# A hybrid DeltaNet/Conformer layer: scan output copied out of PSUM before its norm, and one short convolution for all sample rows

## What is computed

```
proj = rmsnorm(x, g_mix) @ w_in                       # q|k|v, z, b, a, GLU input
qkv  = silu(causal_depthwise_conv([history, q|k|v], w_short))   # width 4, 1536 channels
o, s = gated_delta_rule(l2norm(q), l2norm(k), v, g, beta, s0)   # chunked scan, 8 heads x 64
o    = rmsnorm(o, g_o) * silu(z)                      # norm per head of 64
cv   = silu(group_layernorm(causal_depthwise_conv([history, glu], w_dw)))  # width 31
x    = x + concat([o, cv]) @ w_out                    # then an MLP of width 4096 and a gate
```

## Time and profile before

| | |
|---|---|
| median of 3 runs | 1814.85 us (1811.62 to 1817.52) |
| profiled execution, own time | 1815.31 us |
| its span | 1813.5 us |
| TensorE busy | 1619.3 us, 89% |
| VectorE busy | 1042.2 us, 57% |
| ScalarE busy | 749.3 us, 41% |
| chain that ended last, TensorE's share | 68% |
| mean granted TensorE clock | 0.951 |

### The profile page before, as it was taken

The page is one execution under the profiler, slowest core; times in us unless marked ns, Lnnn a source line. Parts: engine busy times, 40 slices in busy tenths (PEclk is TensorE's granted clock), DMA queues, the critical chain, the costliest instruction groups (busy, mean ns, idle before and its releaser), DMA issues.

```text
span 1813.5 us, 27026 instructions
## 1 busy us (share of the span) xinstructions
PE 1619.3 (89%) x11162; PEld 1405.8 (78%) x11162; DVE 1042.2 (57%) x1707; ACT 749.3 (41%) x1192; POOL 65.6 (4%) x68
## 2 busy tenths in 40 slices
PE   4998866899989997877899999987999999999987
PEld 2786656888978775654677777766989999999987
DVE  3755699678763665779655554455334343434543
ACT  5556523344355424532224243354543242414454
POOL 0000000000000040000000000000000000000000
PEclk9999897899999989888899999999999999999999
DMA  6353222322233332312221213323323333233322
GB/s 181 87 146 102 66 79 65 84 81 77 65 104 82 78 87 68 90 47 64 59 68 45 65 52 91 98 83 117 101 83 93 88 88 94 82 94 87 92 70 82
DMA packets 281023, 153.33 MB, mean 85 GB/s; under 512 B 36996, under 2 KB 272636, under 8 KB 280893
## 3 DMA queue, kind: packets, MB, share of 16 engines
q1 hardware_dynamic: 279879, 150.32, 29.3%
q10 hardware_dynamic: 1022, 1.28, 0.3%
HBM read 135.03 MB, written 16.97 MB: 84 GB/s over the span
## 4 chain that ended last, share of the span: by engine, by line
PE 68%; DVE 16%; ACT 8%; issue 4%; DMA 3%; ACTq 0%; SPq 0%; POOL 0%; DVEq 0%; POOLq 0%
PE ps L1299 55%; DVE of L1964 3%; DVE prod L1883 3%; PE ps L1435 2%; DVE Xp L1884 2%; DVE w_lo L1634 2%; PE ps L1464 2%; PE ps L1458 1%; PE ps L1413 1%; DVE tk L1856 1%; ACT L919 1%; DMA w_raw<-in_w_up 1%; PE ps L1282 1%; PE ps L1425 1%; ACT w_hi L915 1%
## 5 line engine op out<-in xcount | busy, mean ns | idle before, releaser
L915 ACT ACTIVATE w_hi<-w_raw 128x1024 fp32r<-128x1024 f32 (+3 forms) x258 | 232.6, 902 | 320.1 <-DMA w_raw<-in_w_down 175.8
L1299 PE MATMUL ps<-hh_hi,w_hi 128*128 128x256 f32 (+1 forms) x960 | 322.4, 336 | 29.0 <-DVE w_lo L1634 23.2
L1299 PE MATMUL ps<-hh_lo,w_hi 128*128 128x256 f32 (+1 forms) x960 | 314.9, 328 | 0.0
L1299 PE MATMUL ps<-hh_hi,w_lo 128*128 128x256 f32 (+1 forms) x960 | 314.3, 327 | 0.0
L1634 DVE TENSOR_TENSOR w_lo<-w_raw,w_hi 128x1024 fp32r<-128x1024 f32 (+3 forms) x258 | 266.7, 1034 | 55.1 <-ACT w_hi L915 54.3
L1299 PE MATMUL ps<-u_hi,w_hi 128*128 128x512 f32 (+2 forms) x768 | 260.3, 339 | 28.6 <-DVE w_lo L1634 14.2
L1299 PE MATMUL ps<-u_lo,w_hi 128*128 128x512 f32 (+2 forms) x768 | 252.7, 329 | 0.0
L1299 PE MATMUL ps<-u_hi,w_lo 128*128 128x512 f32 (+2 forms) x768 | 252.2, 328 | 0.0
L1299 PE MATMUL ps<-hm_hi,w_hi 128*128 128x512 f32 (+5 forms) x600 | 211.1, 352 | 27.2 <-ACT yb L961 9.8
L1299 PEld LDWEIGHTS ps<-hh_hi,w_hi 128*128 128x128 f32 x960 | 184.8, 193 | 52.9 <-DVE w_lo L1634 34.1
L1299 PE MATMUL ps<-hm_lo,w_hi 128*128 128x512 f32 (+5 forms) x600 | 201.1, 335 | 0.0
(11 more groups left out here) (274 smaller groups left out, 2254.1 us busy)
## 6 DMA issues: line engine op xcount, KB each, us to landing
w_raw<-in_w_up SPq DMA_DIRECT2D x64, 512.0 KB, 4.0
w_raw<-in_w_in SPq DMA_DIRECT2D x48, 512.0 KB, 4.2
w_raw<-in_w_down SPq DMA_DIRECT2D x64, 256.0 KB, 2.7
w_raw<-in_w_down SPq DMA_DIRECT2D x32, 512.0 KB, 4.0
w_raw<-in_w_out SPq DMA_DIRECT2D x16, 512.0 KB, 4.0
w_raw<-in_w_ple_gate SPq DMA_DIRECT2D x16, 512.0 KB, 4.1
qt<-qkv_dram SPq DMA_DIRECT2D x8, 768.0 KB, 5.2
xin<-in_x_prompt SPq DMA_DIRECT2D x8, 512.0 KB, 6.3
```

What stands on the lines that cost most here:

```text
L915: nc.scalar.activation(w_hi[job.slot][:, 0:job.kts, 0:job.m], w_raw[job.slot][:, 0:job.kts, 0:job.m], ACT.Copy).then_inc(w_hid, 1)
L1299: last = nc.tensor.matmul(dst, wt[job.slot][:, k, 0:m], x[:, k, lo:hi], start=(i == 0 and n == 0), stop=(end and n == 2), skip_group_check ...
```

## The change

**The norm.** In `gsq` ACT now copies the tile's output from PSUM to `onr` in head order, waits for that copy (`o_copied`), and squares `onr` from SBUF. In `gno` DVE multiplies `onr` in place. TensorE's first state-times-Q product of the next tile, which overwrites the output's banks, waits for the copy and no longer for the norm.

**The samples' short convolution.** ACT copies the 32 sample columns of a q|k|v block straight to `raws` (history and new rows of all 12 blocks), and no longer to `raw` and `yb`. DVE's per-block short convolution covers only the 512 prompt tokens. A new stage `sv` does all 12 blocks at once: four products and three sums over 128 x 384 (`sy`, `spr`), one copy of the new history, a Silu on ACT, and one DMA of 12 x 32 columns. It stands where `dc` of block 0 stood; that one moves to the slot of block 1's. `dc` now waits for the DMA of `sy`.

```diff
+    put(half("qkv", 1, QT - 1) + 7, "sv")
     for p in range(CT):
-        put(half("ga", 1, p) + 3, "dc", p)
+        put(half("ga", 1, max(p, 1)) + 3, "dc", p)
...
+            def spill_samples():
+                sp.wait_ge(s_silu, 1)
+                sp.dma_start(qkv_dram.rearrange("(k p) t -> p k t", p=P)[:, :, SEQ:TOK],
+                             sy[:, :, :, :].rearrange("p k b t -> p k (b t)")).then_inc(s_st, 16)
...
-                nc.scalar.activation(raw[j % 2][:, QH + lo:QH + hi], src, ACT.Copy)
-                nc.scalar.activation(yb[n][:, lo:hi], src, ACT.Copy, scale=wsh[:, SC - 1, j:j + 1]).then_inc(freed(job, c), 1)
+                end = min(hi, HALF)
+                nc.scalar.activation(raw[j % 2][:, QH + lo:QH + end], src[:, 0:end - lo], ACT.Copy)
+                if hi > HALF:
+                    nc.scalar.activation(raws[:, j, :, QH:], src[:, HALF - lo:].rearrange("p (b t) -> p b t", b=DB), ACT.Copy).then_inc(s_in, 1)
+                nc.scalar.activation(yb[n][:, lo:end], src[:, 0:end - lo], ACT.Copy, scale=wsh[:, SC - 1, j:j + 1]).then_inc(freed(job, c), 1)
...
+            def sample_silu():
+                act.wait_ge(s_conv, 1)
+                nc.scalar.activation(sy[:, :, :, :], sy[:, :, :, :], ACT.Silu).then_inc(s_silu, 1)
...
                 act.wait_ge(o_mm, GATE[t] + 1)
-                src = ps[:, 4:6, 0:PR * HD] if t < NT else ps[0:NS, 4:5, 0:2 * PR * HD]
-                nc.scalar.activation(sqt[0:n, 0:DW].rearrange("p (a b) -> p a b", a=1 if t == NT else 2), src, ACT.Square).then_inc(o_sq, 1)
+                wait(act, o_tr, GATE[t])
...
+                nc.scalar.activation(dst, src, ACT.Copy).then_inc(o_cp, 1)
+                act.wait_ge(o_cp, GATE[t] + 1)
+                nc.scalar.activation(sqt[0:n, 0:DW], onr[0:n, :], ACT.Square).then_inc(o_sq, 1)
...
                 if b == 0:
-                    wait(pe, o_n, GATE[t])
+                    wait(pe, o_cp, GATE[t])
...
                 for k in range(QH):
-                    if s and k == 0:
-                        step(nc.vector.tensor_copy(raws[:, j, :, QH:QH + DS], x[:, QH + HALF:].rearrange("p (b t) -> p b t", b=DB)))
-                        nc.vector.tensor_copy(tail[:, j, 0:QH], x[:, HALF:HALF + QH])
-                        nc.vector.tensor_copy(tail[:, j, QH:].rearrange("p (b r) -> p b r", b=DB), raws[:, j, :, DS:DS + QH])
-                    elif k == 0:
-                        nc.vector.tensor_copy(qh[:, j, :], x[:, HALF:HALF + QH])
-                    if s:
-                        nc.vector.scalar_tensor_tensor(out=ys, in0=raws[:, j, :, k:k + DS], scalar=w(k), in1=ys, op0=ALU.mult, op1=ALU.add)
+                    if k == 0:
+                        nc.vector.tensor_copy(tail[:, j, 0:QH] if s else qh[:, j, :], x[:, HALF:HALF + QH])
...
+            def sample_conv():
+
+                dve.wait_ge(s_in, QT)
+                for n in range(2):
+                    dve.wait_ge(st_yb[n], 16 * spills(1, "qkv")[n])
+                ys, pr = sy[:, :, :, :], spr[:, :, :, :]
+                for k in range(SC):
+                    w = bc(bc(wsh[:, k, :], 2, DB), 3, DS)
+                    step(nc.vector.tensor_tensor(pr if k else ys, raws[:, :, :, k:k + DS], w, ALU.mult))
+                    if k and k < SC - 1:
+                        step(nc.vector.tensor_tensor(ys, ys, pr, ALU.add))
+                nc.vector.tensor_tensor(ys, ys, pr, ALU.add).then_inc(s_conv, 1)
+                nc.vector.tensor_copy(tail[:, :, QH:].rearrange("p j (b r) -> p j b r", b=DB), raws[:, :, :, DS:DS + QH]).then_inc(s_conv, 1)
...
                 dve.wait_ge(o_r, g + 1)
-                wait(dve, o_tr, g)
...
+                nc.vector.tensor_tensor(heads(onr[0:n, :]), heads(onr[0:n, :]), bc(ss[0:n, 0:H], 2, HD), ALU.mult).then_inc(o_n, 1)
...
             def sample_taps(p):
-                for n in range(2):
-                    dve.wait_ge(st_yb[n], 16 * spills(1, "qkv")[n])
+                dve.wait_ge(s_st, 16)
```

More of the change, by code:

```diff
@@ L486, in build @@
         cn = at(TR, "cn", [P, TS[1]], off=4416 + 3 * 2176)
+        sy = at(TR, "sy", [P, QT, DB, DS], off=4416)
+        spr = at(TR, "spr", [P, QT, DB, DS], off=4416 + 2176)
         hm = [[at(M0, f"hm{s}_{n}", [P, KT, TS[s]], F32R, off=32768 * s + 32 * TS[s] * i)
@@ L522, in build @@
         onr = at(MX, "onr", [P, DW])
+        o_cp = sem("o_copied")
         sqt = at(MX, "sqt", [P, DW])
@@ L588, in build @@
         hg_tr, hq_tr = sem("glu_hist_tr"), sem("qkv_hist_tr")
+        s_in, s_conv, s_silu, s_st = (sem(n) for n in ("sample_rows", "sample_conv", "sample_silu", "sample_st"))
         d_ug, d_mm, d_exp, d_msk = sem("d_ug"), sem("d_mm"), sem("d_exp"), sem("d_msk")
@@ L698, in spill @@
                 t0 = HALF * s
-                sp.dma_start(dram[j * P:(j + 1) * P, t0:t0 + TS[s]], yb[n][:, 0:TS[s]]).then_inc(st_yb[n], 16)
+                w = HALF if kind == "qkv" else TS[s]
+                sp.dma_start(dram[j * P:(j + 1) * P, t0:t0 + w], yb[n][:, 0:w]).then_inc(st_yb[n], 16)
             def spill_qkv(s, j):
@@ L719, in load_qt @@
                 if t == NT:
+                    sp.wait_ge(s_st, 16)
                     sp.wait_ge(st_h, 32)
@@ L815, in store_y @@
                 sp.dma_start(rows_of(o["y_p"][0], o["y_s"], i), yrow[e % 2][0:tokens_of(i)[0], :]).then_inc(st_y[e % 2], 16)
-            stages = {"spq": spill_qkv, "spz": spill_z, "qt": load_qt, "zt": load_zt, "pr": store_pairs, "lp": load_pairs,
+            stages = {"spq": spill_qkv, "spz": spill_z, "sv": spill_samples, "qt": load_qt, "zt": load_zt, "pr": store_pairs, "lp": load_pairs,
                       "tt": store_inverses, "tl": load_inverses, "xr": load_rows, "s0": load_states, "ss": store_state,
@@ L1070, in silu @@
             def silu(s, j):
-                rows = yb[spilled("qkv", s, j)[0]][:, 0:TS[s]]
+                rows = yb[spilled("qkv", s, j)[0]][:, 0:HALF]
                 act.wait_ge(y_done, s * QT + j + 1)
                 nc.scalar.activation(rows, rows, ACT.Silu).then_inc(silu_done, 1)
+            def sample_silu():
+                act.wait_ge(s_conv, 1)
+                nc.scalar.activation(sy[:, :, :, :], sy[:, :, :, :], ACT.Silu).then_inc(s_silu, 1)
             def squares(t):
@@ L1122, in gate_square @@
                 act.wait_ge(o_mm, GATE[t] + 1)
-                src = ps[:, 4:6, 0:PR * HD] if t < NT else ps[0:NS, 4:5, 0:2 * PR * HD]
-                nc.scalar.activation(sqt[0:n, 0:DW].rearrange("p (a b) -> p a b", a=1 if t == NT else 2), src, ACT.Square).then_inc(o_sq, 1)
+                wait(act, o_tr, GATE[t])
+                if t < NT:
+                    dst, src = onr[:, :].rearrange("p (q r e) -> p r q e", r=2, e=HD), ps[:, 4:6, 0:PR * HD].rearrange("p r (q e) -> p r q e", e=HD)
+                else:
+                    dst, src = onr[0:NS, :], ps[0:NS, 4, :]
+                nc.scalar.activation(dst, src, ACT.Copy).then_inc(o_cp, 1)
+                act.wait_ge(o_cp, GATE[t] + 1)
+                nc.scalar.activation(sqt[0:n, 0:DW], onr[0:n, :], ACT.Square).then_inc(o_sq, 1)
             def gate_rms(t):
@@ L1218, in _ @@
                       "dk": decays, "sc": norms, "bk": back, "uw": inverse_times, "gsq": gate_square, "gno": gate_rms,
-                      "sp": sample, "cv": norm_square, "cr": norm_root, "cs": norm_out, "op": operand, "hq": qkv_history,
+                      "sp": sample, "cv": norm_square, "cr": norm_root, "cs": norm_out, "op": operand, "hq": qkv_history, "sv": sample_silu,
                       "hg": glu_history, "st": stats, "pe": p_rows, "yr": last_norm, "y": y_rows}
@@ L1556, in qkv_history @@
                 pe.wait_ge(y_done, 2 * QT)
+                pe.wait_ge(s_conv, 2)
                 for g in range(3):
@@ L1704, in short_conv @@
                 w = lambda k: wsh[:, k, j:j + 1]
-                ys = y[:, HALF:HALF + NS].rearrange("p (b t) -> p b t", b=DB)
                 for k in range(QH):
-                    if s and k == 0:
-                        step(nc.vector.tensor_copy(raws[:, j, :, QH:QH + DS], x[:, QH + HALF:].rearrange("p (b t) -> p b t", b=DB)))
-                        nc.vector.tensor_copy(tail[:, j, 0:QH], x[:, HALF:HALF + QH])
-                        nc.vector.tensor_copy(tail[:, j, QH:].rearrange("p (b r) -> p b r", b=DB), raws[:, j, :, DS:DS + QH])
-                    elif k == 0:
-                        nc.vector.tensor_copy(qh[:, j, :], x[:, HALF:HALF + QH])
-                    if s:
-                        nc.vector.scalar_tensor_tensor(out=ys, in0=raws[:, j, :, k:k + DS], scalar=w(k), in1=ys, op0=ALU.mult, op1=ALU.add)
+                    if k == 0:
+                        nc.vector.tensor_copy(tail[:, j, 0:QH] if s else qh[:, j, :], x[:, HALF:HALF + QH])
                     ins = nc.vector.scalar_tensor_tensor(out=y[:, 0:HALF], in0=x[:, k:k + HALF], scalar=w(k), in1=y[:, 0:HALF],
@@ L2014, in _ @@
```

(2 more changed lines are left out.)

## The result

| | median us | executions |
|---|---|---|
| before | 1814.19 | 4 (1811.62 to 1817.52) |
| changed | 1826.99 | 4 (1820.26 to 1828.47) |
| changed / before | 1.0062 | 95% interval 1.0032 to 1.0092 |

The forecast was 1819.4 with a range up to 1824.0: too low, and "same" where the median is 0.6% slower. One of the third comparison's nine executions took 3059.83 us and is not in its ratio.

The account below looks back on a forecast made before the run. TensorE, busy 89% of the span, was taken to bound the kernel, so only its waits count. Terms -2.8 + 0.1 + 3.3 + 2.3 + 1.7 = +4.6 us on the median 1814.85 gave 1819.4 us, range 1811.5 to 1824.

Parts of the forecast that it names:

- same: Whole kernel: a time within 0.3% (5.4 us) of before, 1809.4 to 1820.3 us; chance 0.58.
- The moved taps: In the slot of dc 1, DVE also does block 0, so Vn comes 1.6 us late: +1.7 us, bounds 1.2 and 2.5.
- the stall: Near 490 us TensorE waits for ACT's sigmoid eviction behind the samples' Silu: +3.3 us, range 2.3 to 4.7.
- Half clock behind the stall: After TensorE's wait near 490 us, a stretch at 1.2 GHz in place of 2.4: +2.3 us, bounds 0 and 2.6.
- The norm: Product moves ahead of the norm wait, 3.9 us gained in six tiles, ACT's copy costs some back: -2.8 us, from 0 to -3.9.
- The old short convolution: DVE's samples' operations removed from each of 12 q|k|v blocks: nobody waits for them, zero.
- the third ACT copy: A 32-column copy added in each q|k|v block, mattering only at the 1.1 us late-eviction wait: +0.1 us.
- The level: Base of the forecast: the difference was added to the median 1814.85 us of the kernel before.
- kinder: Rival: no low clock behind the new wait, or none at tiles 4 and 6; 1813.5 to 1817 us, chance 0.22.
- The strided operations: Rival: the new stage's seven DVE operations at prd's ratio or above, 1.4 to 3 us longer, 1820.5 to 1823; chance 0.15.
- A table switch's drain: Rival: 1.4 us idle behind each ACT table load, 2.8 us more, 1822 us; chance 0.02.
- The whole norm wait goes: Rival: transposes meet a finished norm, 13.3 us go in place of 3.9; 1810.0 us or less, 1806 with clock; chance 0.06.

Follow-up runs that it names:

- third comparison: The changed kernel, unedited, timed once more against the kernel before: 1.0040 (1.0024 to 1.0056), +7.3 us.
- changed again: The changed kernel, unedited, timed a second time against the kernel before: 1.0034 (1.0021 to 1.0047), +6.2 us; profiled span 1823.0.
- convolution alone: The kernel before with only the short convolution's part of the change, norm as before: 1.0057 (1.0037 to 1.0076), +10.4 us.
- Silu later: The changed kernel with ACT's samples' Silu and SP's DMA one job later, against the kernel before: 1.0016 (1.0001 to 1.0031), +2.9 us.
- taps alone: The kernel before with only the samples' dc of block 0 moved to block 1's slot: 1.0021 (1.0007 to 1.0034), +3.8 us.
- first profile: Profiled execution of the unedited changed kernel, its fastest of four when first measured: 1820.26 us, span 1818.5.
- scored comparison: The changed kernel's first measurement against the kernel before, four executions each: 1826.99 against 1814.19 us, 1.0062 (1.0032 to 1.0092).
- norm-alone profile: The kernel before with only the norm's part of the change (ACT copy, square from onr, product waiting for the copy): 0.9994 (0.9979 to 1.0009), -1.1 us.
- the kernel with both moves: The changed kernel with samples' Silu and DMA one job later and dc of block 0 ahead of block 1's: 0.9997 (0.9985 to 1.0009), -0.5 us.
- the kernel with late transposes: The kernel before with the norm's part and the norm's transposes queued behind the next chunk's last product: 0.9921 (0.9895 to 0.9947), -14.4 us.
- the stall alone: The changed kernel with dc of block 0 apart and the samples' Silu left in place, against the kernel before: 1.0019 (1.0006 to 1.0032), +3.5 us.

## Why the prediction was wrong, step by step

- **The moved taps, "+1.7 us; bounds 1.2 and 2.5": the step that failed.** The wait was sized rightly (1.59 against 1.6), but no clock was put behind it, and no reason was given, though the same text did so for the stall. In the five other profiles that have this wait (changed again and third, convolution alone, Silu later, taps alone) TensorE fell to 1.2 GHz for 6.8 us within 1.3 us of its end, and the term measured 4.7 to 4.8 us: 1.6 to 1.7 of wait and 3.1 of clock. The rows ahead of the forecast went both ways: products at full speed after waits of 1.29 to 1.98 us, and a slow one after 1.97. In the first profile the term came out, at 1.8; its whole span was 5.0 us longer where +4.6 was forecast. So the failed step does not show in that execution, and whether it is what made the three slower ones of the scored comparison slow is not known, since they were not profiled.
- **Half clock behind the stall, "+2.3 us; bounds 0 and 2.6": right in mechanism and about right in size.** It lasted 3.4 us in the first profile and 6.8 in the four others with the stall, and cost 1.4 and 2.6 to 2.7 us by the table. That is less than half of its length, 1.7 and 3.4.
- **The stall, +3.3: right**, in each of its prices. The Silu behind DVE's stage, with the sigmoid's table to reload, is its cause, since it goes when the Silu moves; how much of it is the wait for DVE and how much the reload was not parted by a run.
- **The norm, -2.8: right in mechanism, too high.** The waits moved as forecast. From the matmul 30 places ahead of the transposes to the transposes themselves, the norm-alone profile is shorter than the one before by 3.5 us over the six tiles, against 3.9 forecast; it is 0.5 longer at the samples' norm (0.5 forecast) and 0.7 longer behind tile 7 (0.6). Not in the sum was `u_lo`, 1.1 us given back in tile 5. That leaves about 1.2; the median gave 1.1, with an interval of 2.7 to either side.
- **The old short convolution and the third ACT copy, 0 and +0.1: not contradicted**, by the kernel with both moves, which keeps them and stands where the norm's part stands, with intervals of some 2 us. TensorE's wait on the late eviction in 350 to 480 us is 1.1 us in it, as before.
- **The level.** The forecast added to 1814.85, the median of three. In some 70 later executions the kernel before had medians of 1817.9 to 1818.2 and ranged from 1809.95 to 1825.07. If the scored comparison stands at the same level, which no run tests, some 3 us of the 7.6 by which the forecast was low belong to the three runs, 2 to the change, and the rest to the scatter of four executions. Three of the four executions of before in the scored comparison are those three runs, so it has nearly the same low level. The range allowed for terms of the sum, and for nothing of this.
- **The rivals.** The clock was put in as kinder only; it was the other way behind the taps. The strided operations were not dear: 0.56 us each. A table switch's drain did not appear: the eviction starts 0.01 us after its load (490.39 against 489.10 + 1.28), so the Trainium skill's 1.38 us in ScalarE: Activation LUTs, "What ACT_TABLE_LOAD costs", has no counterpart here. "The whole norm wait goes" was rightly small for this change, and rightly priced: the kernel with late transposes won 14.4 us, between the waits' own 13.3 and the 4 more that the forecast gave to the clock (1810.0 to 1806).

**What stays open.** The half clock between 538 and 556 us comes in all seven profiles that have the stall or the wait on `Vn`, one of them (the stall alone) with no wait on `Vn`, and not in those of before, of the norm alone and of both moves; waits of 1.5, 0.6 and 3.1 us stand just ahead of it, and are in the profile before too. In the first profile and in that of the stall alone it begins inside the 3.1 us wait. But the kernel with late transposes, which has nothing of the convolution's part and runs some 10 us ahead there, has it too, at the same matmuls:

```profile
514.00:531.00 17.00, 11.83 (x62) 0.93 0.51 179
531.00:565.00 34.00, 31.97 (x168) 0.98 0.26 73
```

So neither of the change's waits is needed for it, and it is not counted to the taps here; whether they make it more frequent was not told apart. By the last two columns of the table it is worth 2.5 us where it lasts 6.8 and 1.6 to 1.7 where it lasts 3.4. Open too is why the first comparison's other three executions took 1826 to 1828: the third profile (1829.0 span) shows that the kernel can, with 16.5 us more at half clock than the first profile, 9.7 of them outside 480 to 556 us.

## What to carry to other kernels

Put the clock's price behind every new wait, not behind the largest: here a wait of 1.6 us cost 4.7 us with the clock behind it in five profiles of six. When a wait is taken off an instruction, look at the next one in the queue with the same condition: moving the transposes a slot later, behind the chunk's last product, was worth 13 us, where removing the product's wait was worth 1. And where a batched stage needs another engine in its middle, give each engine its own place in the order; the batching cost nothing that could be told once the Silu stood behind the eviction and the taps stood apart.

## What was not expected of the hardware

- TensorE's clock differs from one execution to the next of one kernel with the same waits: 184.3 us at half clock within the span in the first profile of the changed kernel, 184.2 in the second and 200.8 in the third, with the stretches at other places. The total does not tell the time: the second is 4.5 us longer than the first with the same total, and 3.3 of these arise between 480 and 556 us, where it has 17.0 us at half clock and the first 10.2.
- 29 executions of the unchanged kernel in one comparison ran from 1809.95 to 1822.26 us, 0.7%. A forecast to 0.3% needs more than three runs of its base.
